# Prompt scores from high and low f16 parts, one rotation for both key sets, and another bank for the turned pooling columns

## The reference

```
h = rms_norm(xp, g_pre_mix[l])
z = h @ w_in                                   # 1024 -> 512 q, 3 x 256 k and v, 24 gates, 512 pooling columns
q = rope(z[..., :ATT_W].reshape(B, T, N_HEADS, HEAD_DIM), pos)
kv_s = rope_kv(z[..., OFF_KVS:OFF_KVW]...)     # keys and values of the selected branch
kv_w = rope_kv(z[..., OFF_KVW:OFF_GATE]...)    # of the window branch
u = z[..., OFF_POOL:]                          # input of the pooling group
...
s = jnp.einsum('tghd,tgkd->tghk', q, ks) * SCALE
o_sel = jnp.einsum('tghk,tgkd->tghd', masked_softmax(s, m_sel), vs)
...
s = jnp.einsum('tghd,kgd->tghk', q, kw[:, 0]) * SCALE
o_win = jnp.einsum('tghk,kgd->tghd', masked_softmax(s, m_win), kw[:, 1])
```

## Time and profile before

| | |
|---|---|
| median of 3 runs | 1612.02 us (1611.85 to 1615.12) |
| the profiled execution | 1615.65 us |
| its span, first to last instruction | 1613.9 us |
| mean granted TensorE clock | 0.958 of full |
| busy: PE, DVE, ACT, POOL | 1475.5, 710.7, 549.8, 398.1 us |

### The profile page before, as it was taken

One profiled execution on the slowest core, in us unless ns is written; L12 is line 12 of the kernel. 1 busy time (PEld: TensorE's weight loads), 2 busy tenths in 40 slices (PEclk: granted clock), 3 DMA queues, 4 the chain that ended last, 5 costly groups with the idle time before them and its releaser, 6 DMA issues.

```text
span 1613.9 us, 25175 instructions
## 1 busy us (share of the span) xinstructions
PE 1475.5 (91%) x10052; PEld 871.1 (54%) x10052; DVE 710.7 (44%) x1217; ACT 549.8 (34%) x1188; POOL 398.1 (25%) x459
## 2 busy tenths in 40 slices
PE   6488997977999979998989999999999999999995
PEld 3244553544444446654445666666666665666664
DVE  5799994675678736665552111111111121100103
ACT  5133224545566636663332221222221221111103
POOL 2243423676567620003210111111111110000004
PEclk9799997978999989998998999999999999999998
DMA  9666643000000066672111111111111121121102
GB/s 375 218 213 208 204 136 113 2 1 1 1 1 1 1 267 261 284 236 79 52 45 53 28 51 52 52 52 47 31 52 52 52 68 40 37 71 36 36 14 111
DMA packets 93475, 146.58 MB, mean 91 GB/s; under 512 B 3691, under 2 KB 74831, under 8 KB 91143
## 3 DMA queue, kind: packets, MB, share of 16 engines
q1 hardware_dynamic: 81823, 78.43, 15.6%
q0 software_dynamic: 11520, 67.11, 11.6%
q10 hardware_dynamic: 56, 0.01, 0.0%
HBM read 135.91 MB, written 14.04 MB: 93 GB/s over the span
## 4 chain that ended last, share of the span: by engine, by line
PE 59%; DVE 2%; ACT 1%; DMA 1%; POOL 1%; issue 0%; DVEq 0%; POOLq 0%; ACTq 0%
PE psum L1677 45%; PE psum L1644 6%; PE psum L1195 2%; PE psum L1207 2%; PE psum L1233 1%; PE psum L1255 1%; DMA arena<-in_cache_kv_sel,sel_idx 1%; PE psum L796 1%; DVE arena L1865 1%; POOL arena L1630 0%; ACT arena L1329 0%; PE psum L1655 0%; PE psum L1262 0%; PE psum L1713 0%; PE psum L1211 0%
## 5 line engine op out<-in xcount | busy, mean ns | idle before, releaser
L1677 PE MATMUL psum<-arena 128*128 128x384 f16 (+1 forms) x4752 | 734.2, 318 | 5.4 <-POOL arena L1627 2.8
L1677 PEld LDWEIGHTS psum<-arena 128*128 128x128 f16 x4752 | 466.1, 98 | 273.1 <-issue 9.7
L1942 DVE SCALAR_TENSOR_TENSOR arena<-psum,arena 128x384 f32<-128x384 f32 (+1 forms) x66 | 35.3, 535 | 349.5 <-ACT arena L1796 349.5
L1627 POOL TENSOR_TENSOR arena<-arena 128x384 f32 (+1 forms) x66 | 57.6, 872 | 464.8 <-ACT arena L1798 464.8
L2269 PE MATMUL psum<-arena 128*128 128x512 f16 (+1 forms) x768 | 155.6, 364 | 0.0
L1796 ACT ACTIVATE arena<-psum 128x384 f32<-128x384 f32 (+1 forms) x66 | 31.2, 472 | 338.5 <-PE psum L1677 338.5
L1106 POOL TENSOR_TENSOR arena<-arena 128x768 f32<-128x768 f32 (+3 forms) x96 | 131.2, 1380 | 5.0
L983 ACT ACTIVATE arena<-psum,arena 128x384 f32<-128x384 f32 (+3 forms) x192 | 104.5, 552 | 55.7 <-DVE arena L1021 22.4
L2269 PEld LDWEIGHTS psum<-arena 128*128 128x128 f16 x768 | 76.8, 100 | 74.6 <-issue 7.8
L2052 POOL DMA_INDIRECT arena<-in_cache_kv_cmp,cmp_idx x64 | 78.5, 1226 | 147.6 <-DVE arena L2200 108.8
L916 PE MATMUL psum<-arena 64*128 64x384 f32 (+3 forms) x384 | 88.3, 540 | 17.3 <-ACT arena L983 11.4
(11 more groups left out here) (266 smaller groups left out, 1559.6 us busy)
## 6 DMA issues: line engine op xcount, KB each, us to landing
arena<-in_w_gate SPq DMA_DIRECT2D x22, 512.0 KB, 4.0
arena<-in_w_up SPq DMA_DIRECT2D x22, 512.0 KB, 5.2
arena<-in_w_down SPq DMA_DIRECT2D x8, 1408.0 KB, 7.0
arena<-in_x_prompt SPq DMA_DIRECT2D x16, 512.0 KB, 3.7
arena<-in_w_in SPq DMA_DIRECT2D x8, 908.0 KB, 11.9
arena<-in_cache_kv_win SPq DMA_DIRECT2D x8, 512.0 KB, 3.5
out_y_prompt<-arena SPq DMA_DIRECT2D x8, 512.0 KB, 2.6
out_kv_win_sample<-in_cache_kv_win SPq DMA_DIRECT2D x1, 4032.0 KB
```

What stands on the lines that cost most here:

```text
L1627: nc.gpsimd.tensor_tensor(row(1), silu_out[c][:, 0:c1 - c0], row(0), ALU.subtract).then_inc(act_ready, 1)
L1677: ins = pe.matmul(out[:, 0:c1 - c0], w[wp][:, k, :], x[xp][:, k, c0:c1], start=(k == 0 and i == 0), stop=(k == n_k - 1 and i == 2))
```

## The change

1. Queries and both key sets are kept as two f16 parts in the same memory: the high part is the f16 copy, the low part what is left. ScalarE writes the high parts of the queries and (new) of the keys; VectorE subtracts them from the turned values in PSUM and writes the low parts, in place of its two copies of turned keys. The sample tile's queries stay f32; its keys are added together again by POOL.
2. A prompt score is three f16 products, added up in PSUM (high x high, high x low, low x high), the two groups alternating, in place of one f32 product; so are the scores against compressed keys.
3. Selected and window keys are rotated together by `rotate_keys`, where the selected keys alone stood before.
4. The turned pooling columns go to bank 3 (the bank of `zu`), in the last tile to bank 5. The turn no longer waits for the saved queries; the `zu` product waits for the saved pooling columns, and the turn of the queries for the queries of the tile before.

```diff
-        ksT = keep(TILES * P)
-        kwT = keep(TILES * P)
+        qT_half = qT.rearrange("p t j n -> p (t j n)").bitcast(F16).rearrange("p (t h j n) -> p t h j n", t=TILES, h=2, j=HPG)
+        kT_half = keep(2 * TILES * P).bitcast(F16).rearrange("p (h c t n) -> p h c t n", h=2, c=2, t=TILES)
...
+        SPLIT = ((0, 0), (0, 1), (1, 0))
...
-                        ins = pe.matmul(B[:, c:c + G * NC_P], qT[:, NT - 1 - 2 * m - x, j, :],
-                                        ckT_p.rearrange("p g n -> p (g n)"), start=True, stop=True)
+                        for i, (qp, kp) in enumerate(SPLIT):
+                            ins = pe.matmul(B[:, c:c + G * NC_P], qT_half[:, NT - 1 - 2 * m - x, qp, j, :],
+                                            ckT_half[:, kp].rearrange("p g n -> p (g n)"), start=(i == 0), stop=(i == 2))
...
-                ins = nc.vector.tensor_copy(ckT_p[r, g, :], B[r, 0:NC_P])
+                ins = nc.vector.tensor_copy(ckT_half[r, 0, g, :], B[r, 0:NC_P])
+            step(ins)
+            for g in range(G):
+                r = slice(g * HD, (g + 1) * HD)
+                ins = nc.vector.tensor_tensor(ckT_half[r, 1, g, :], B[r, 0:NC_P], ckT_half[r, 0, g, :], ALU.subtract)
...
-                for g in range(G):
-                    r = slice(g * HD, (g + 1) * HD)
-                    ins = pe.matmul(bank(2 * (x.n % 2) + g)[:, 0:x.nb * P], qT[r, NT - 1 - u.i, x.j, :], kT[r, c:c + x.nb * P], start=True, stop=True)
+                for i, (qp, kp) in enumerate(SPLIT):
+                    for g in range(G):
+                        r = slice(g * HD, (g + 1) * HD)
+                        ins = pe.matmul(bank(2 * (x.n % 2) + g)[:, 0:x.nb * P], qT_half[r, NT - 1 - u.i, qp, x.j, :],
+                                        kT_half[r, kp, 1 if u.kind == "sel" else 0, k0:k0 + x.nb, :].rearrange("p t n -> p (t n)"),
+                                        start=(i == 0), stop=(i == 2))
...
-                nc.scalar.activation(qT[:, bass.ds(row, 1), :, :].rearrange("p a j n -> p (a j) n"), qT_ps, ACT.Copy, scale=SCALE).then_inc(qT_saved, 1)
-
-                act.wait_ge(k_roped, t + 1)
+                if t == NT:
+                    nc.scalar.activation(qT[:, row, :, :], qT_ps, ACT.Copy, scale=SCALE).then_inc(qT_saved, 1)
+                else:
+                    nc.scalar.activation(qT_half[:, row, 0, :, :], qT_ps, ACT.Copy, scale=SCALE).then_inc(q_high, 1)
+
+                act.wait_ge(kT_done, t + 1)
+                nc.scalar.activation(kT_half[:, 0, :, t, :], kT_ps[:, 0:2, :], ACT.Copy).then_inc(k_high, 1)
...
+            def rotate_keys(tab):
+                half = ROT // 2
+                x = zs[:, KVR:3 * KVR].rearrange("p (k r) -> p k r", k=2)[:, :, 0:KV].rearrange("p k (g d) -> p k g d", g=G)
...
+                nc.vector.tensor_tensor(ra, x[:, :, :, 0:ROT], over(tab[:, 0:ROT], ROT), ALU.mult)
+                nc.vector.tensor_tensor(rb[:, :, :, 0:half], x[:, :, :, half:ROT], over(tab[:, ROT:ROT + half], half), ALU.mult)
+                step(nc.vector.tensor_tensor(rb[:, :, :, half:ROT], x[:, :, :, 0:half], over(tab[:, ROT + half:2 * ROT], half), ALU.mult))
+                nc.vector.tensor_tensor(x[:, :, :, 0:ROT], ra, rb, ALU.add).then_inc(k_roped, 1)
...
-                dve.wait_ge(z_copied, 4 * t + 2)
-                dve.wait_ge(q_roped, t + 1)
-                rotate(zs[:, 2 * KVR:2 * KVR + KV].rearrange("p (h d) -> p h d", h=G), tab, G)
...
-                rotate(zs[:, KVR:KVR + KV].rearrange("p (h d) -> p h d", h=G), tab, G, k_roped)
+                dve.wait_ge(q_roped, t + 1)
+                rotate_keys(tab)
...
-                dve.wait_ge(kT_done, t + 1)
-                nc.vector.tensor_copy(kwT[:, bass.ds(t * P, P)], kT_ps[:, 0, :])
-                nc.vector.tensor_copy(ksT[:, bass.ds(t * P, P)], kT_ps[:, 1, :]).then_inc(kT_saved, 1)
+                if t < NT:
+                    dve.wait_ge(q_high, t + 1)
+                    nc.vector.scalar_tensor_tensor(qT_half[:, NT - 1 - t, 1, :, :], qT_ps, SCALE, qT_half[:, NT - 1 - t, 0, :, :],
+                                                   ALU.mult, ALU.subtract).then_inc(qT_saved, 1)
+                dve.wait_ge(k_high, t + 1)
+                nc.vector.tensor_tensor(kT_half[:, 1, :, t, :], kT_ps[:, 0:2, :], kT_half[:, 0, :, t, :], ALU.subtract).then_inc(kT_saved, 1)
...
                     project(zkc, s, ATT, 2 * KVR)
+                    pe.wait_ge(uT_saved, t + 1)
                     project(zu, s, ATT + ZKV, PW)
                 pe.wait_ge(q_roped, t + 1)
-                pe.wait_ge(uT_saved, t + 1)
+                if t:
+                    pe.wait_ge(qT_saved, t)
...
-                pe.wait_ge(qT_saved, t + 1)
                 for j in range(4):
-                    ins = pe.transpose(qT_ps[:, j, :], uz[:, j * P:(j + 1) * P], ident)
+                    ins = pe.transpose((uT_ps if t < NT else uT_last_ps)[:, j, :], uz[:, j * P:(j + 1) * P], ident)
```

More of the change, by code:

```diff
@@ L1112, in prompt_pool @@
                 nc.gpsimd.tensor_copy(v_new[0:NS, c, 1:KV + 1], z_all[0:NS, NT, c0 + KV:c0 + 2 * KV])
[L1113 to L1114 removed]
+            for c in range(2):
+                ins = nc.gpsimd.tensor_tensor(kT_new[:, c, :], kT_half[:, 0, 1 - c, NT, 0:NS], kT_half[:, 1, 1 - c, NT, 0:NS], ALU.add)
+            ins.then_inc(new_saved, 1)
             aside = Paced(setup_pool(pool, step))
```

18 lines of the change are left out of this document (11 added, 7 removed).

## The result

The changed kernel takes 1594.28 us in the median of 4 runs (1593.74 to 1595.11), the kernel before 1611.93 beside it (1610.38 to 1615.12), with a ratio of 0.9877 (0.986 to 0.9895). The two medians are 17.7 us apart; the ratio is not their quotient, and it comes to about 20 us. The prediction said 1604 with a range from 1597 to 1614. The same two kernels, run again later, gave 1593.51 and 1615.04, 21.5 us apart, ratio 0.9869 (0.9854 to 0.9885). The profiled execution of the change took 1594.73 us with a span of 1592.9, 21.0 less than the span before.

A forecast was written before the change was run, and what follows sets the result against it. TensorE was taken to bound the prompt attention, VectorE the projection. Scores -9.6, compressed-key split +0.2, projection +0.7 and ScalarE's copy +0.4 gave -8.3 us: 1607.3 from the profiled execution, 1604 forecast from the median, range 1597 to 1614.

The forecast's parts named there:

- Scores, width: Prompt scores: three column times instead of four per group, both halves at once, extra loads hidden; saves 14.1 us of TensorE work.
- Rival (a): Prompt scores: pairs of f16 products do not run at once, six column times instead of four; 1638 us; 6%.
- rival (b): Prompt scores: weight loads stand open, two openings of about 0.1 us per group, 17.6 us against 14.1 saved; 1616 us; 9%.
- Scores, fixed part: Prompt scores: the 0.20 us per group independent of width stays; a shorter load trims some 0.05 us, 4 us at most.
- Compressed scores: Scores against compressed keys: 64 f32 instructions become 96 f16 ones, bound by weight loads; 0 us, bounds 1.5 either way.
- The share that arrives: Prompt attention: of 14.1 us saved on TensorE, 0.5 + 3.8 + 5.3 = 9.6 us shorten the time.
- what the split of the compressed keys costs: Compressed keys: two small VectorE subtractions and one wait, 0.4 us once, half of it on the path: +0.2 us.
- Rival (c): Prompt attention: VectorE's two-column step, held by POOL, sets the exponential's start; the loop absorbs the gain; 1608 us; 17%.
- Projection: Nine token tiles: VectorE's net per tile +0.1 us, about +1 in all; +0.7 us after a saved TensorE wait, bounds -0.5 and +3.
- ScalarE's new copy: End of the last projection tile: the high key copy goes before the save of the pooling columns, +0.4 us.
- The base: Starting time for the sum: the median of 1612.02 us, instead of the profiled execution of 1615.65, which stood 3.6 above it.

The follow-up runs named there:

- the fourth product: The changed kernel with a fourth f16 product, low x low, in each prompt score: 1606.42 us, ratio 0.995 to the kernel before.
- by the halves: The kernel before with each f32 prompt score cut into two products of half the columns: 1617.87 us, ratio 1.0024 to the kernel before.
- the rotation with the bank: The kernel before with only the combined key rotation and the pooling columns' second bank, no f16 parts: 1608.13 us, ratio 0.9966.
- the subtractions with the bank: The changed kernel with the two key rotations kept apart, f16 parts and bank kept: 1597.86 us, ratio 0.9895 to the kernel before.

## Why the prediction was wrong, step by step

**Scores, width: right.** Three column times instead of four for each group, both halves at once, no open loads after the first, as the 0.16 us for 128 columns and the 0.17 us of the fourth product show. Rival (a) had asked for 1.0 us or more at 384 columns, rival (b) for 0.85 to 0.9; it is 0.59, and the order of the halves makes no difference. The rule of the Trainium skill ("TensorE: Matmul & The Clock Gate", Part 3, The mechanism) that I had weighed against the earlier trace rows would have had the second and third loads of each half stand open; the traces do not agree with it, by that 0.17 us. The same section also lets a load into a background weight buffer be pulled ahead, and the traces do not contradict that.

**Scores, fixed part: the step that failed.** I wrote "I keep the 0.20 us fixed" and gave a shorter load at most 0.05 us a group, 4 us in all. It fell by 0.09, in 96 groups 8.6 us of TensorE's work, and so twice the most that I allowed. It is paid once in a group; my reading is that it holds the first weight load, which has nothing to hide behind, and that in f16 with 128 columns this load is much shorter. The loads come at 114 ns in f32 and at 60 in f16 with 127 columns, where they set the pace, and at 29 or less in f16 with 128. 114 - 29 = 85 ns is near the 0.09 us that the change gained, 60 - 29 = 31 ns near the 0.04 that 127 columns gave back, and 114 - 60 = 54 ns near the 0.05 left between those two. That these are one exposed load is worked out from the spacings and not shown; that the load's speed is in the fixed part is shown by the 127 columns, and that it comes once by the halves.

**Compressed scores: the second failure, the larger in proportion.** I took 0 with bounds of 1.5 us either way: "more of them but each shorter". No price of a load stands behind that 0; the only one that I had, 0.1 us in rival (b), is the length of one record in the earlier trace rows. In a row of loads the price is the spacing, and it is at most 29 ns against 114: f16 took the block from the pace of its loads down to that of its columns. The term was -4.5 us by the blocks and -6 to -7 by the kernel with f32 in its place. What could have told it was there: sixteen in 1.83 us are 114 ns each, while the record of an f32 load is 196 ns long, so records overlap.

**The share that arrives: somewhat less than I had.** I let 9.6 of 14.1 us arrive, 68%. TensorE saves 40 x 0.25 + 20 x 0.31 + 28 x 0.20 + 8 x 0.14 = 22.9 us. Of the 19.9 us by which the stage shrank, the f32 compressed scores give back 6.7, and 13.3 are left (327.13 against 313.87) for the prompt scores, 58%. The 13.3 hold what the split of the compressed keys costs, which I had at +0.2. My 68% of the right size would have been 15.6, so the share that was too high hid 2.3 us of the miss. Where it arrives differs from what I wrote: the group that starts at 407.48 us before starts at 399.54 in the kernel that has f32 compressed scores, and from the first score on that is 156.45 against 149.47, 7.0 us where I had 4.3 (0.5 + 3.8). I had 5.3 for the rest, which brings 6.3. The timeline of before and of that kernel:

```profile
407.48 1.13 PE L916 MATMUL psum<-arena 64*128 64x512 f32 x4
```

```profile
399.54 0.82 PE L924 MATMUL psum<-arena 64*128 64x512 f16 x6
```

**Rival (c): a real mechanism, with the wrong weight.** The waits for the exponentials went to 25.4 us, beyond the 24 at which I had said that it is (c), and yet the gain came. They grew to what I had set as its sign because more was saved, not because the saving was lost: between four products and three 9.2 to 9.7 of 14.1 us arrive in the attention, so there TensorE still sets the pace for the most part; between three and one only 1.4 to 1.8 of 28.2 do, with longer waits and a lower clock. The wait of the two-column step for POOL is there; it costs 0.7 to 1.9 us of the attention at three products and up to 6.9 at one. The Trainium skill ("SBUF — State Buffer", SBUF: two separate sides) has this as an exclusive lock for VectorE with two SBUF inputs; 0.16 us with POOL idle, 0.81 until its end, and 0.34 with a scalar operand while it multiplies agree.

**Projection: right in kind, 1.4 us off.** Per tile I had 0.68 + 0.40 + 0.65 for the new steps and a net of +0.1. Measured: 0.94 for the two subtractions, 0.63 for the combined rotation, net 0.94 + 0.63 - 0.62 - 0.62 - 0.40 = -0.07, so -0.6 us over eight tiles and not +0.8. The stage came out at -0.3 against +1.1 (or +0.7 for TensorE alone); over the nine kernels that have this projection the first score starts between 249.84 and 250.98 us, so -0.3 is at the high end and -1.0 more usual. VectorE's time passes to TensorE nearly whole there: -5.1 for the rotation with the bank and +3.5 for the subtractions with the bank. That is -1.6 with the bank counted twice, and what the bank is worth by itself was not run. ScalarE's new copy delays the save of the pooling columns by 0.35 us, as predicted (0.4).

**The base.** I moved the sum from the profiled 1615.65 us to the median of three runs, 1612.02, which took 3.6 us off the forecast; the runs since put the median at 1615. That error went the other way and hid part of the miss: by its own sum the forecast was 1607.3, 13 us above what came. The span shrank by 21.0 where the sum has 8.3; of the 12.7 us between them 6.7 are the compressed scores, 3.9 the prompt scores with the split of the compressed keys (9.4 against 13.3), 1.4 the projection, and 0.8 fell behind the attention.

## What to carry to other kernels

Where small products change type, price their weight loads by the spacing in a place where loads set the pace, not by the length of one record, and look at what a group costs on entry as well as by the column. When an engine is the bound and a loop is nearly as long, ask how far a saving goes before the loop takes it: here two thirds of it arrived between four products and three, and a twentieth between three and one. Compare the granted clock too, since an engine that waits more may be slower in its other work. And look for a small VectorE step with two SBUF operands that stands behind POOL's long ones: here a scalar operand made it independent of POOL for the price of one more instruction.

## What the runs showed of the hardware

- In blocks of 64-column products weight loads of 128 columns come every 114 ns in f32 and every 29 ns in f16, where the columns alone need 27; with 127 columns every 60 ns in f16. One column fewer in the scores cost 6 to 7 us in this kernel.
- A score group split over the two row halves costs 0.11 us beside its columns in f16 and 0.20 in f32, nearly whatever the number of products in it (0.12 with four f16 ones instead of three; 0.86 against 0.84 us in all when the f32 ones were doubled) and, in f16, whatever their order.
- A rotation of four VectorE instructions over 32 to 64 elements took 0.63 us, one over half as many 0.62: at this size the time does not depend on the elements. The two subtractions of 256 and 512 elements took 0.41 and 0.69 us.
- The two-column step of VectorE with both operands in SBUF took 0.160 us at the least and 1.445 at the most of 32; as two instructions with a scalar operand 0.203 to 0.215 each.
- TensorE's mean clock in the attention was 0.93 with three products and 0.87 with one: with 28.2 us less to do at full clock it was busy only 17.4 us less.
